# A decoder trunk on one Trainium2 core: two additions of the last residual on GpSimd, one store for two chunks, mask rows repeated by transfers

## The reference

```python
# dsa_block: keys outside the top-k get no weight
score = einsum('bths,bth->bts', relu(raw), wi) * IDX_HEADS ** -0.5
_, idx = lax.top_k(where(visible, score, -inf), topk)
logits = einsum('btgrd,btkgd->btgrk', qg, k_sel) * Dh ** -0.5
prob = softmax(where(valid, logits, -inf));  o = einsum('btgrk,btkgd->btgrd', prob, v_sel)
# trunk, end of each layer; f is the output of the second SwiGLU
x = x + 0.5 * m[8] * rmsnorm(f, g_post[l, 2])
```

## Time and profile before

| | |
|---|---|
| runs | 1341.39, 1342.2 and 4134.66 us, median 1342.2 |
| the profiled execution | 1341.61 us |
| its span on the core | 1339.9 us |
| PE busy | 1314.6 us, 98% of the span |
| VectorE busy | 777.9 us, 58% |
| ScalarE busy | 623.9 us, 47% |
| GpSimd busy | 115.4 us, 9% |
| DMA | 259.42 MB, 194 GB/s on average |
| granted TensorE clock | 1.0 of full |

### The profile page before, as it was taken

The page is one execution under the profiler, slowest core; times in us unless marked ns, Lnnn a source line. Parts: engine busy times, 40 slices in busy tenths (PEclk is TensorE's granted clock), DMA queues, the critical chain, the costliest instruction groups (busy, mean ns, idle before and its releaser), DMA issues.

```text
span 1339.9 us, 24410 instructions
## 1 busy us (share of the span) xinstructions
PE 1314.6 (98%) x9774; PEld 1242.9 (93%) x9774; DVE 777.9 (58%) x1444; ACT 623.9 (47%) x1074; POOL 115.4 (9%) x207
## 2 busy tenths in 40 slices
PE   6999999999999999999999999999999999999998
PEld 4999999989976889999998999999988989999997
DVE  5544444578886875455456644545578895444443
ACT  5433334354544664344445543434478664443333
POOL 1100000023011130000001100000030120000000
PEclk9999999999999999999999999999999999999999
DMA  9865646449469746644644555454566734444442
GB/s 378 303 213 192 213 167 236 158 149 300 142 247 367 301 144 221 209 141 144 224 153 153 213 164 194 143 191 142 166 226 209 281 112 142 144 153 147 130 147 86
DMA packets 78497, 259.42 MB, mean 194 GB/s; under 512 B 10208, under 2 KB 20048, under 8 KB 77248
## 3 DMA queue, kind: packets, MB, share of 16 engines
q1 hardware_dynamic: 61520, 197.97, 43.6%
q0 software_dynamic: 16736, 59.44, 12.2%
q10 hardware_dynamic: 144, 0.66, 0.1%
HBM read 253.80 MB, written 4.23 MB: 193 GB/s over the span
## 4 chain that ended last, share of the span: by engine, by line
PE 88%; DVE 6%; DMA 2%; issue 1%; ACT 1%; SPq 0%; POOL 0%; DVEq 0%; ACTq 0%
PE ps L1760 28%; PE ps L1762 27%; PE ps L1761 27%; PE ps L1833 2%; DMA front<-in_front 2%; DVE w_lo L2341 1%; DMA w_raw<-in_ada 1%; DVE f L2426 1%; DVE f L2409 1%; PE ps L1377 1%; DVE x L2413 0%; DVE f L2431 0%; DVE xn_lo L2421 0%; PE ps L876 0%; DVE xf_o L2537 0%
## 5 line engine op out<-in xcount | busy, mean ns | idle before, releaser
L1760 PE MATMUL ps<-xn_hi,w_hi 128*128 128x320 f32 x1800 | 564.4, 314 | 7.5 <-DVE xn_lo L2421 4.6
L1762 PE MATMUL ps<-xn_hi,w_lo 128*128 128x320 f32 x1800 | 556.2, 309 | 0.0
L1761 PE MATMUL ps<-xn_lo,w_hi 128*128 128x320 f32 x1800 | 556.1, 309 | 0.0
L2341 DVE TENSOR_TENSOR w_lo<-w_raw,w_hi 128x1024 fp32r<-128x1024 f32 (+1 forms) x357 | 382.1, 1107 | 112.0 <-ACT w_hi L2113 111.5
L2113 ACT ACTIVATE w_hi<-w_raw 128x1024 fp32r<-128x1024 f32 x362 | 331.0, 959 | 76.5 <-PE ps L1762 70.9
L1760 PEld LDWEIGHTS ps<-xn_hi,w_hi 128*128 128x128 f32 x1800 | 337.9, 188 | 23.6 <-issue 10.8
L1761 PEld LDWEIGHTS ps<-xn_lo,w_hi 128*128 128x128 f32 x1800 | 338.0, 188 | 0.4
L1762 PEld LDWEIGHTS ps<-xn_hi,w_lo 128*128 128x128 f32 x1800 | 337.9, 188 | 0.0
L1760 PE MATMUL ps<-mid_hi,w_hi 128*128 128x320 f32 x704 | 218.0, 310 | 0.3 <-DVE w_lo L2341 0.3
L1761 PE MATMUL ps<-mid_lo,w_hi 128*128 128x320 f32 x704 | 217.3, 309 | 0.0
L1762 PE MATMUL ps<-mid_hi,w_lo 128*128 128x320 f32 x704 | 217.2, 309 | 0.0
(11 more groups left out here) (347 smaller groups left out, 1027.0 us busy)
## 6 DMA issues: line engine op xcount, KB each, us to landing
w_raw<-in_gu SPq DMA_DIRECT2D x176, 512.0 KB, 4.8
a_raw<-in_ada POOLq DMA_DIRECT2D x72, 512.0 KB, 6.9
w_raw<-in_down SPq DMA_DIRECT2D x64, 512.0 KB, 3.6
w_raw<-in_pj SPq DMA_DIRECT2D x57, 512.0 KB, 4.9
w_raw<-in_down SPq DMA_DIRECT2D x64, 192.0 KB, 3.6
ex_xn<-in_ada POOLq DMA_DIRECT2D x16, 512.0 KB, 6.2
w_raw<-in_ada SPq DMA_DIRECT2D x12, 512.0 KB, 12.1
front<-in_front SPq DMA_DIRECT2D x5, 1024.0 KB, 14.3
```

The costliest lines, as they stand in the source:

```text
L1760: pe.matmul(out, hi, xhi, start=start, stop=False)
L1761: pe.matmul(out, hi, xlo, start=False, stop=False)
L1762: return pe.matmul(out, w_lo[s][:, w_at:w_at + P], xhi, start=False, stop=stop)
L2341: dve.tensor_tensor(w_lo[s][:, cols], w_raw[:, s, cols], w_hi[s][:, cols].bitcast(F32), ALU.subtract).then_inc(w_split, 1)
```

## The change

**Mask rows.** The two matmuls (four instructions in the trace) and ScalarE's copy are gone. In their place GpSimd, right after the stores of head 1, waits for the finished mask, stores `bias_s` four times to a scratch tensor in DRAM, once for each query head, waits for these, and loads `bias_r` from there in one transfer. VectorE's `soft` of unit 8 waits for that transfer. PE's wait for the states moves to the logits of unit 9, the next writer of those banks.

**Tail.** GpSimd adds chunks 2 and 4. VectorE scales chunk 0, then 1 and 2, 3 and 4, chunk 5 alone, 6 and 7 together, and adds 6 and 7 in one operation. PE's chunk 5 waits for six scaled chunks. SyncE stores chunks 6 and 7 in one transfer of 320 KB, last.

```diff
+        def repeat_bias(gp):
+            gp.wait_ge(bias_ready, 3)
+            for r in range(NR):
+                gp.dma_start(bias_rows[:, r, :, :], bias_s[:, :]).then_inc(rows_out, 16)
+            gp.wait_ge(rows_out, 16 * NR)
+            gp.dma_start(bias_r[:, :, :], bias_rows.rearrange("(a b) r t n -> (b r t) a n", a=2)).then_inc(rep_ready, 16)
...
                 store_states(gp, h)
+                if h == RH - 3:
+                    repeat_bias(gp)
...
                 elif u == N_PU + 1:
-                    pe.wait_ge(rep_ready, 1)
+                    pe.wait_ge(st_ready, RH)
...
                 else:
-                    pe.wait_ge(bias_ready, 3)
-                    pe.wait_ge(st_ready, RH)
-                    for bh in range(2):
-                        last = pe.matmul(ps[:, bh, 0:KEYS_S], rep_s[:, bh, :], bias_s[:, :], start=True, stop=True)
-                    last.then_inc(rep_done, 1)
                     turn(N_PU - 1)
...
-                else:
-                    act.wait_ge(rep_done, 1)
-                    act.activation(bias_r[:, :, :], ps[:, 0:2, 0:KEYS_S], ACT.Copy).then_inc(rep_ready, 1)
...
                 if u == N_PU:
-                    dve.wait_ge(rep_ready, 1)
+                    dve.wait_ge(rep_ready, 16)
...
             store_y(0, y_added, 1)
-            store_y(2, x_ready, 8 * 5 + 1)
+            store_y(2, gp_added, 1)
             store_y(1, y_added, 2)
-            store_y(4, x_ready, 8 * 5 + 2)
+            store_y(4, gp_added, 2)
             store_y(3, y_added, 3)
             store_y(5, y_added, 4)
-            store_y(6, x_ready, 8 * 5 + 3)
-            store_y(7, x_ready, 8 * 5 + 4)
+            sp_.wait_ge(x_ready, 8 * 5 + 2)
+            sp_.dma_start(t["y"][6:8].rearrange("k p n -> p k n"), x[:, 6:8, :]).then_inc(out_done, 16)
...
-                    pe.wait_ge(y_grown, k + 1 + k % 2)
+                    pe.wait_ge(y_grown, k + 1 + (k % 2 if k < 5 else 0))
...
             grow_out(0, 1)
             grow_out(1, 2)
-            add_out(2, 3)
             grow_out(3, 2)
-            add_out(4, 5)
-            grow_out(5, 2)
-            add_out(6, 7)
+            grow_out(5, 1)
             dve.wait_ge(f_whole, 8 * SUB["down3"] + 1)
-            grow_out(7, 1)
-            add_out(7, 8)
+            grow_out(6, 2)
+            dve.wait_ge(y_grown, KC)
+            dve.tensor_tensor(x[:, 6:8, :], x[:, 6:8, :], f[:, 6:8, :], ALU.add).then_inc(x_ready, 2)
...
             gp.wait_ge(odd_stored, 32)
+            for k, grown in ((2, 3), (4, 5)):
+                gp.wait_ge(y_grown, grown)
+                gp.tensor_tensor(x[:, k, :], x[:, k, :], f[:, k, :], ALU.add).then_inc(gp_added, 1)
```

More of the change, by code:

```diff
@@ L414, in build @@
         x_ready = sem("x_ready")
+        gp_added = sem("gp_added")
         sqx_ready = sem("sqx_ready")
@@ L515, in build @@
         o_ready = sem("o_ready")
-        rep_done, rep_ready = sem("rep_done"), sem("rep_ready")
+        rows_out, rep_ready = sem("rows_out"), sem("rep_ready")
+        bias_rows = nc.dram_tensor("bias_rows", (NB, NR, NT, KEYS_S), F32).ap()
         lg_done, lg_ready, exp_ready, pr_ready = sem("lg_done"), sem("lg_ready"), sem("exp_ready"), sem("pr_ready")
@@ L1745, in _ @@
             store_y(0, y_added, 1)
-            store_y(2, x_ready, 8 * 5 + 1)
+            store_y(2, gp_added, 1)
             store_y(1, y_added, 2)
-            store_y(4, x_ready, 8 * 5 + 2)
+            store_y(4, gp_added, 2)
             store_y(3, y_added, 3)
             store_y(5, y_added, 4)
-            store_y(6, x_ready, 8 * 5 + 3)
-            store_y(7, x_ready, 8 * 5 + 4)
-            sp_.wait_ge(out_done, 16 * KC)
+            sp_.wait_ge(x_ready, 8 * 5 + 2)
+            sp_.dma_start(t["y"][6:8].rearrange("k p n -> p k n"), x[:, 6:8, :]).then_inc(out_done, 16)
+            sp_.wait_ge(out_done, 16 * (KC - 1))
         @block.tensor
@@ L2748, in grow_out @@
                                   ps[:, B_RY, 0:TOK].unsqueeze(1).to_broadcast([P, n, TOK]), ALU.mult).then_inc(y_grown, n)
-            def add_out(k, grown):
-                dve.wait_ge(y_grown, grown)
-                dve.tensor_tensor(x[:, k, :], x[:, k, :], f[:, k, :], ALU.add).then_inc(x_ready, 1)
             grow_out(0, 1)
             grow_out(1, 2)
-            add_out(2, 3)
             grow_out(3, 2)
-            add_out(4, 5)
-            grow_out(5, 2)
-            add_out(6, 7)
+            grow_out(5, 1)
             dve.wait_ge(f_whole, 8 * SUB["down3"] + 1)
-            grow_out(7, 1)
-            add_out(7, 8)
+            grow_out(6, 2)
+            dve.wait_ge(y_grown, KC)
+            dve.tensor_tensor(x[:, 6:8, :], x[:, 6:8, :], f[:, 6:8, :], ALU.add).then_inc(x_ready, 2)
         @block.gpsimd
```

## The result

The changed kernel takes 1343.2 us (median of 22 runs, 1342.57 to 1346.24). The kernel before, run beside it, takes 1341.39 us (median of 22, lowest 1341.1, with the one of 4134.66 that stands alone). The ratio is 1.0015 with a 95% interval of 1.0009 to 1.0022: slower by 0.15%, some 2 us. In every kernel some executions take about 3 us more than the rest (1344.49 and 1344.7 are two of the kernel before), in unequal numbers, which shifts the ratios and widens their intervals, so medians stand beside them here.

A forecast was written before the change was run, and what follows sets the result against it. The prediction took TensorE (PE) to bound the kernel, with 88% of the chain. It summed -0.39 (PE's gain), +0.2 (DMA crowding) and -0.49 (tail) to -0.7 us, so 1340.9 us, range 1339.4 to 1343.2.

The forecast's parts named there:

- the part on the tail, GpSimd: After the last down projection: GpSimd's additions of chunks 2 and 4 take 0.88 us each and cost nothing.
- The sum: Whole kernel: PE's gain, DMA crowding and the tail's stores together give -0.7 us, so 1340.9 us.
- Attention, PE's gain: Last head of attention: without mask matmuls, unit 7's transposes wait only for VectorE's division and start earlier, -0.39 us.
- Attention, the crowding: Attention, 417 to 424 us: mask transfers on GpSimd's queue delay the load of w_raw and so PE, +0.2 us.
- rival B: Attention: DMA crowding makes the load of w_raw late by the full 0.95 us, so 1341.7 us; chance 0.20.
- the rule of the Trainium skill: DMA engines alternate between queues packet by packet; with 1,280-byte rows against 4,096, the stretch to 421.6 would cost 0.23 us.
- Attention, the round trip: Mask stores land near 424.4, the load of bias_r near 431, 3.6 us before the soft step needs it.
- C: Attention: the soft step waits for the mask's round trip, 1.8 us later, so 1342.9 us; chance 0.12.
- Tail: After the last down projection: last store starts 0.98 us earlier, its double size costs 0.49 more, net -0.49 us.
- Rival D: Tail: the large store needs about 0.9 us more or GpSimd's additions hold SyncE's queue, so 1341.3 us; chance 0.14.

The follow-up runs named there:

- experiment 2: The kernel before the change with only the new tail, mask rows made by PE and ScalarE as before: 1342.91 us, 1.0012.
- Experiment 1: The changed kernel with VectorE instead of GpSimd adding chunks 2 and 4: 1340.75 us, 0.9999 against the kernel before.
- experiment 4: The kernel before the change with GpSimd only waiting for the last scaling at the end of its program: 1344.97 us, 1.0034.
- experiment 5: The kernel before the change with only the mask rows repeated by transfers, tail as before: 1341.55 us, 0.9998.

## Why the prediction was wrong

**The step that failed** is in the part on the tail, GpSimd: "Their store slots are at about 1333.9 and 1335.0, so they cost nothing." The slots were right, and nobody waited for the additions. But their cost was counted only as far as their readers. GpSimd had been done at 1104.8; with the additions its program ends at 1334.24, and the drain goes on for 6.63 us after that. That ends 2.2 us after SyncE's own drain (1340.9 against 1338.7). Of these 6.63 us 0.33 come with the mask's five transfers (6.30 without them in experiment 2), so the other half of the change has a part in the loss after all, by way of the drain. Experiment 1 takes the additions away and the span becomes 2.1 us shorter; experiment 4 adds nothing but the late end and the span becomes 3.3 us longer. The row that would have told it stood in the trace before: a DRAIN of 6467 ns on GpSimd, 7 ns on SyncE. No term of the prediction looked at the closing line, since nobody waits for GpSimd there in the kernel before.

**The sum.** Forecast were -0.39 + 0.2 - 0.49 = -0.7 us. Without the drain the changed kernel's SyncE ends 1.0 us earlier (1338.7 against 1339.7). With it, the span is 1.2 us longer. The medians differ by 1.8: 0.3 of that lies outside the span and is unexplained, and 0.3 is the profiled execution's place among the others.

**Attention, PE's gain** (-0.39): from the states of head 3 to the soft step it takes 435.00 - 430.74 = 4.26 us in the kernel before and 434.50 - 430.65 = 3.85 after, so -0.41; so do all the other traces (experiment 5). Right, and for the reason given: the transposes follow the division (it ends at 432.87, they start at 432.92).

**Attention, the crowding** (+0.2): this term was sized wrong, without harm to the outcome. From the finished mask to those states it took 13.60 us before and 430.65 - 416.92 = 13.73 after, but the kernels with and without the transfers spread over the same 13.6 to 13.7 (experiment 5), so the cost is nothing that shows. PE's wait for `w_raw` became 0.3, where 0.2 stood and 0.4 was forecast. The queues between 417 and 424, after:

```profile
q1 hardware_dynamic: 658, 2.40, 84.8%
q0 software_dynamic: 226, 0.48, 18.0%
```

GpSimd's queue rose from 13.4 to 18.0%, SyncE's fell from 88.6 to 84.8%, far from the 66.9 of rival B. But these seven microseconds hold two different stretches. The shares of each, SyncE's queue and then GpSimd's:

| stretch | before | after |
|---|---|---|
| 417.7 to 421.6 | 97.8%, 4.7% | 97.0%, 6.1% |
| 421.6 to 424.0 | 84.8%, 16.8% | 73.8%, 27.1% |

The first packet of mask rows starts at 421.47 in the trace, though the first store was issued at 417.70, and the load of `w_raw`, issued at 407.73, had landed by 421.5, 13.8 us later where 13.9 stood. So the mask rows travelled after the load that they were to delay: the term took them to be on the way from 417.7, or from 420. PE's wait is 0.1 longer because PE came 0.2 earlier, not because the load came later. For the same reason the 0.23 us worked out by the rule of the Trainium skill (DMA: Bandwidth & Descriptors, Queues, rings and completion order) for the 1.6 us to 421.6 was put to no test here; the packets of mask rows were also 5,120 bytes in size, and not 1,280. Together the stage gained 0.41 us where 0.19 was forecast. The rest of the 0.50 by which the soft step is earlier in the changed kernel's trace is scatter between executions: the finished mask lies at 416.70 to 417.18 in the kernels with the old mask.

**Attention, the round trip.** The stores were issued 417.70 to 419.4 as forecast and landed 5.3 to 6.6 us later, not 5.0; the load was issued at 426.29 instead of 424.4 and landed at 432.6 instead of 431. It had 1.9 us to spare, not 3.6. Right, but nearer to C than I thought; C itself didn't happen, and that the time came out near C's 1342.9 is chance.

**Tail.** GpSimd's addition takes 0.87 us (0.88 by the line through two sizes). The last store is issued 1336.10 - 1337.6 = -1.5, of which -0.48 came with the start of the tail, so -1.02 for -0.98. It lands after 2.4 us as forecast. Net -0.5: right. Rival D named GpSimd's additions, but by holding up SyncE's queue, which they didn't: ScalarE's chunk 5 is there at 1335.70, and that is what the last stores follow.

## What to carry to other kernels

An engine that has long been idle isn't free at the end of a program: where its last instruction lies decides when it can close. Before work is moved to such an engine in the last 10 us, look up the DRAIN of the closing line for each engine and add it behind the new last instruction; here GpSimd had to be done some 6.3 to 6.6 us before the last store landed, whatever it did. And a gain of half a microsecond in one stage is read from the distance between two instructions around it, in several traces, since the times of a kernel of 1341 us don't tell 0.5 us apart. A share of a queue is read over the stretch in which both kinds of traffic are on their way, and not over a window around it.

## What the runs showed of the hardware

- GpSimd's closing DRAIN goes on for 6.28 to 6.30 us after its last operation, DMA issue or bare wait, and for 6.63 in the kernels with the mask's transfers; on the other engines the whole of it takes 0.007 us (SyncE) to 1.7 us (PE's weight loads).
- It grows with the number of transfers that GpSimd has issued, by 0.065 us each over twenty small loads and over five mask transfers, and not with the number of its computing instructions.
- Mask rows whose stores GpSimd issued from 417.70 on, while SyncE's queue held 97% of the DMA time, began to move at 421.47.
- The view of waits ascribed SyncE's last 2.4 us to PE, whose own drain had ended 5.6 us before: the engine named there isn't always the one that was late, and the windows with no engine and no DMA busy are the surer sign.
- One output store of 320 KB lands 2.4 us after its issue, two of 160 KB 1.9 us after theirs, one slot of 0.5 us apart: merging the last two neither gained nor cost anything that shows (1340.75 against 1340.65 us).
